# Router logits in column groups during the mixer, a gather into feature rows, four modulation tiles in the second block, and another chain behind the experts

## What is computed

```python
x = x + ada_x[2][:, None, :] * yx                                # end of the mixer
hx2 = modulate(rmsnorm(x, norm_ffn_g[l]), ada_x[3], ada_x[4])    # h * (1 + scale) + shift
aff = softmax((h @ w_router).astype(float32), axis=-1)           # 16 experts
gate, idx = lax.top_k(swapaxes(aff, 1, 2), cap)                  # cap = 32 tokens of each expert
xg = h[bidx, idx]
a, b = xg @ w1[e], xg @ w3[e]
ye = ((silu(a) * b) @ w2[e]) * gate[..., None]
x = x + ada_x[5][:, None, :] * zeros_like(h).at[bidx, idx].add(ye)
x = rmsnorm(x, final_norm_g)                                     # end of the first block
ada = silu(c) @ w_ada[l] + b_ada[l]                              # second block, l = 0, 1
h = rms_norm(x, norm_mix[l]) * (1.0 + sc_m) + sh_m
... = split(h @ w_in[l])
```

## Time and profile before

| | |
|---|---|
| runs | 2255.99, 2257.81, 2257.02 us; median 2257.02 |
| profiled execution | 2254.84 us, of it 2253.0 in the span |
| mean granted TensorE clock | 0.927 |
| busy | PE 1889.1, PEld 1264.7, DVE 744.3, ACT 334.6 us |
| chain that ended last | PE 59%, DMA 33%, DVE 4%, ACT 2% |
| moved | 648.82 MB, mean 288 GB/s |

### The profile page before, as it was taken

The page is one execution under the profiler, slowest core; times in us unless marked ns, Lnnn a source line. Parts: engine busy times, 40 slices in busy tenths (PEclk is TensorE's granted clock), DMA queues, the critical chain, the costliest instruction groups (busy, mean ns, idle before and its releaser), DMA issues.

```text
span 2253.0 us, 29442 instructions
## 1 busy us (share of the span) xinstructions
PE 1889.1 (84%) x12382; PEld 1264.7 (56%) x12382; DVE 744.3 (33%) x1716; ACT 334.6 (15%) x759; POOL 0.2 (0%) x4
## 2 busy tenths in 40 slices
PE   7999989866666666666666679999999999999999
PEld 4788778411111111111111138868889978688899
DVE  3666243200000000000000034662656546725554
ACT  4132121200000000000000020360110102602100
POOL 0000000000000000000000000000000000000000
PEclk9999999987888878787888899999999999999999
DMA  9356679999999999999999994524645555246441
GB/s 327 114 210 239 224 254 357 405 428 428 428 429 428 429 428 428 428 428 428 428 428 429 428 377 168 186 75 164 230 168 183 186 179 183 76 168 241 152 169 57
DMA packets 148022, 648.82 MB, mean 288 GB/s; under 512 B 10660, under 2 KB 17425, under 8 KB 123158
## 3 DMA queue, kind: packets, MB, share of 16 engines
q1 hardware_dynamic: 144124, 643.78, 72.1%
q10 hardware_dynamic: 3802, 3.65, 0.5%
HBM read 646.36 MB, written 1.05 MB: 287 GB/s over the span
## 4 chain that ended last, share of the span: by engine, by line
PE 59%; DMA 33%; DVE 4%; ACT 2%; issue 1%; SPq 0%; ACTq 0%; DVEq 0%
DMA ring<-in_w_exp 33%; PE bank L2086 15%; PE bank L922 13%; PE bank L2769 6%; PE bank L1869 4%; PE bank L1606 4%; PE bank L2684 3%; PE bank L1884 2%; PE bank L936 1%; PE bank L965 1%; PE bank L800 1%; PE bank L1533 1%; DVE scr L2595 1%; PE bank L963 1%; PE bank L451 1%
## 5 line engine op out<-in xcount | busy, mean ns | idle before, releaser
L1869 PE MATMUL bank<-ring,arena 128*32 128x512 f32 x1968 | 305.2, 754 | 207.9 <-DMA ring<-in_w_exp 197.5
L1869 PEld LDWEIGHTS bank<-ring,arena 128*32 128x32 f32 x1968 | 60.9, 124 | 433.4 <-DMA ring<-in_w_exp 313.5
L922 PE MATMUL bank<-hx,ring 128*128 128x256 f32 x1344 | 293.0, 379 | 0.7 <-ACT hx L818 0.7
L922 PEld LDWEIGHTS bank<-hx,ring 128*128 128x128 f32 x1344 | 254.6, 190 | 37.5 <-issue 3.4
L1884 PE MATMUL bank<-ring,arena 128*32 128x512 f32 x1008 | 161.0, 781 | 78.9 <-DMA ring<-in_w_exp 67.9
L1927 DVE COPY arena<-bank 128x256 f32<-128x256 f32 x16 | 6.8, 425 | 527.2 <-PE bank L1874 527.2
L2086 PE MATMUL bank<-arena 128*128 128x256 f32 x672 | 151.0, 379 | 0.2 <-DVE arena L2135 0.2
L1884 PEld LDWEIGHTS bank<-ring,arena 128*32 128x32 f32 x1008 | 32.9, 132 | 188.7 <-DMA ring<-in_w_exp 107.8
L2086 PEld LDWEIGHTS bank<-arena 128*128 128x128 f32 x672 | 127.0, 190 | 17.5 <-DVE arena L2135 0.6
L1934 DVE COPY arena<-bank 128x256 f32<-128x256 f32 x16 | 6.8, 424 | 344.6 <-PE bank L1758 344.6
L2086 PE MATMUL bank<-ring,hx 128*128 128x256 f32 x448 | 105.8, 379 | 0.0
(11 more groups left out here) (494 smaller groups left out, 2291.2 us busy)
## 6 DMA issues: line engine op xcount, KB each, us to landing
ring<-in_w_exp SPq DMA_DIRECT2D x186, 2048.0 KB, 16.3
ring<-in_w_ada SPq DMA_DIRECT2D x36, 2048.0 KB, 12.8
ring<-in_w_in SPq DMA_DIRECT2D x29, 2048.0 KB, 8.9
ring<-in_w_ffn_in SPq DMA_DIRECT2D x20, 2048.0 KB, 8.0
ring<-in_w_ffn_out SPq DMA_DIRECT2D x10, 2048.0 KB, 7.8
ring<-in_w_out SPq DMA_DIRECT2D x6, 2048.0 KB, 10.8
arena<-in_w_exp SPq DMA_DIRECT2D x4, 2048.0 KB, 19.0
ring<-in_w_up_nsa SPq DMA_DIRECT2D x2, 2048.0 KB, 7.9
```

The costliest lines, as they stand in the source:

```text
L922: ins = pe.matmul(b[:, o:o + n], w[:, k, j * P:(j + 1) * P], h[:, k, :], start=k == 0, stop=k == KD - 1)
L1869: ins = pe.matmul(banks[s][32 * j:32 * j + 32, :], e_xe[:, 2 * t + kk, :], w[:, kk, 512 * j:512 * j + 512], start=t + kk == 0, stop=t + kk ...
```

## The change

- The logits are made from the unnormed xT with gained weights, four chunks at a time in four column groups, the first four during the mixer's output; four partial sums are added when they are turned to tokens. The norm's factor is applied per token behind, by sums of squares with the squares as weights and two columns of ones. Constants of the shift are made early.
- The gather takes token rows as weights and e_ps as the moving side, so that features come out on partitions; ACT's copy and the turn fall away and DVE adds the shift.
- The pairs -2 and -1 leave the router's stage. Pair -2 now stands behind input tile 0 of layer 0; each layer has a pair inside its attention. The pairs are numbered 4l-2 to 4l+1.
- Tiles 4 to 7, 10 and 11 of the first expert have the places outside the ring; 0 to 3 are in the ring, 8 and 9 wait for 0 and 1.
- The last expert is written out of the loop; it has no next gather, its last tile comes in two halves, and its scatter is waited for by pairs of chunks.
- The join makes one norm factor per token from squares as weights and two columns of a weighted vector, spreads it by a diagonal matrix and a matmul, and does the final norm (two matmuls on pre-added squares, `pe_fin`) behind input tile 0.

```diff
     tiles("out1_", wide(A["w_out"][0], 0, D))
-    tiles("late-2_", later[16:18])
-    tiles("late-1_", later[18:20])
     N_PRE = len(stream)
...
-               + wide(w2, QB0, MERGE2))
+        w_first = (wide(w2, 0, KW0) + [(w2[:, KW0:QB0].rearrange("(k p) n -> p k n", p=P), P, KD, QB0 - KW0)]
+                   + wide(w2, QB0, MERGE2))
+        if l:
+            late_tiles(4 * l - 2)
+        for t, ap in enumerate(w_first):
+            after_experts.append((f"in{l}_{t}", ap))
+            if t + l == 0:
+                late_tiles(4 * l - 2)
         merge = wide(w2, MERGE2, IN2)
         for t in range(4):
             if t == 2:
...
+        pe.wait_ge(*at("join weights"))
+        b = bank(pe, "join g")
+        for k in range(KD):
+            pe.wait_ge(*at(f"join square{k}"))
+            for c in range(NC):
+                ins = pe.matmul(b[:, 2 * c:2 * c + 2], sqx[:, k, c * P:(c + 1) * P], j_w[:, k, :], start=k + c == 0, stop=True,
+                                skip_group_check=True)
+        ins.then_inc(*PE.step("full join g"))
+        b = bank(pe, "join scale")
+        for c in range(NC):
+            pe.wait_ge(*at(f"join diagonal{c}"))
+            ins = pe.matmul(b[:, c * P:(c + 1) * P], ones[:, 0:P], j_diag[:, c, :], start=True, stop=True)
+        ins.then_inc(*PE.step("full join scale"))
+
+    def pe_fin(pe):
+        PE.stage("join")
+        pe.wait_ge(*at("fin squares"))
+        b = bank(pe, "join x")
+        for k in range(2):
+            ins = pe.matmul(b[:, 0:N], ones[:, 0:P], sqx[:, k, :], start=k == 0, stop=k == 1)
+        ins.then_inc(*PE.step("full join x"))
+        PE.stage("second")
...
+            act.activation(sqx[:, k, :], xT[:, k, :], ACT.Square).then_inc(*AC.step(f"join square{k}"))
+        act.wait_ge(*at("join eps"))
+        act.wait_ge(*at("full join g"))
+        act.activation(j_root, bank_of("join g")[:, 0:4:2], ACT.Sqrt, bias=j_eps[:, 1:2]).then_inc(
+            *AC.step("free join g", "join root"))
...
+        v.wait_ge(*at("join root"))
+        v.reciprocal(j_rs, j_root).then_inc(*DV.step())
+        v.wait_ge(*DV.last())
+        for c in range(NC):
+            v.tensor_scalar(j_diag[:, c, :], ident[:, :], j_rs[:, c:c + 1], None, ALU.mult).then_inc(*DV.step(f"join diagonal{c}"))
+        v.wait_ge(*at("full join scale"))
         for k in range(KD):
-            v.tensor_tensor(sqx[:, k, :], xT[:, k, :], xT[:, k, :], ALU.mult).then_inc(*DV.step(f"join x square{k}"))
-        v.tensor_tensor(g_join, gs, c_fin[:, 0:8], ALU.mult).then_inc(*DV.step())
...
+            v.scalar_tensor_tensor(sqg[:, k, :], xT[:, k, :], g_join[:, k:k + 1], bank_of("join scale")[:, 0:N], ALU.mult,
+                                   ALU.mult).then_inc(*DV.step("free join scale", f"join scaled{k}"))
+        v.tensor_tensor(sqx[:, 0:4, :], sqx[:, 0:4, :], sqx[:, 4:8, :], ALU.add).then_inc(*DV.step("join halves"))
+        v.wait_ge(*at("join halves"))
+        v.tensor_tensor(sqx[:, 0:2, :], sqx[:, 0:2, :], sqx[:, 2:4, :], ALU.add).then_inc(*DV.step("fin squares"))
...
+                pe_linear_T(pe, f"mixout{p}{t}", f"{wo}{t}", merged, N, 4, None if t else f"merged{p}",
+                            (lambda j: pe_route_early(pe, 4 * t + j)) if p == 0 else None)
...
+    def dve_route_early(v):
+
+        dve_gain(v, "gain ffn0", gs, c_ffn[:, 0:8], adaX[0][:, 32:40], "adaX0b")
+        DV.stage("route")
+        v.wait_ge(*K.loaded("load_moe"))
+        v.wait_ge(*at("full mturn1"))
+        v.memset(e_wrg[:, :, EXPERTS:CAP], 0.0).then_inc(*DV.step())
+        v.tensor_tensor(e_wrg[:, :, 0:EXPERTS], e_wr, spread(gs, 2, EXPERTS), ALU.mult).then_inc(*DV.step("router gained"))
+        v.tensor_tensor(e_wsh, e_wr, spread(adaX[0][:, 24:32], 2, EXPERTS), ALU.mult).then_inc(*DV.step())
+        v.wait_ge(*DV.last())
+        v.tensor_reduce(e_ws, e_wsh.rearrange("p k e -> p e k"), AX, ALU.add).then_inc(*DV.step("router shift"))
+        v.memset(e_eps, EPS).then_inc(*DV.step("eps"))
+        v.memset(e_y, 0.0).then_inc(*DV.step("y zero"))
...
+            DV.stage("route")
+        for k in ((), (1,), (2, 3), (4, 5))[i]:
+            v.wait_ge(*at(f"route square{k}"))
+            if k > 1:
+                v.wait_ge(*DV.last())
+            v.tensor_tensor(e_sq[:, 0, :], e_sq[:, 0, :], e_sq[:, k, :], ALU.add).then_inc(*DV.step("squares summed"))
...
+    def pe_route_logits(pe, r):
+        PE.stage("route")
+        if r == 0:
+            pe.wait_ge(*at("router gained"))
+        for q in range(4):
+            k = 4 * r + q
+            pe.wait_ge(*at(f"x mixed0 {k}"))
+            ins = pe.matmul(bank_of("logits")[32 * q:32 * q + 32, 0:N], e_wrg[:, k, :], xT[:, k, :], start=r == 0, stop=r == 1)
+        ins.then_inc(*PE.step("full logits"))
...
+    def pe_route_early(pe, j):
+
+        stage = PE.cur
+        PE.stage("route")
+        if j == 0:
+            pe.wait_ge(*at("router shift"))
+            b = bank(pe, "router shift")
+            pe.matmul(b[:, 0:EXPERTS], ones[:, 0:P], e_ws, start=True, stop=True)
...
+            ins.then_inc(*PE.step("full router shift"))
+            book.bank["logits"], book.bank["token sums"] = 6, 7
+            claim(pe, 6, "logits")
+            claim(pe, 7, "token sums")
+        elif j == 1:
+            pe_rope(pe)
+        elif j == 5:
+            pe_route_logits(pe, 0)
+        PE.cur = stage
...
+        sums = bank_of("token sums")
+
+        def squares(n, k):
+            for c in range(NC):
+                ins = pe.matmul(sums[:, 2 * c:2 * c + 2], e_sq[:, k, c * P:(c + 1) * P], ones[:, 0:2], start=n + c == 0,
+                                stop=True, skip_group_check=True)
+            return ins
+
+        pe.wait_ge(*at("squares summed"))
+        squares(0, 0)
+        pe_route_logits(pe, 1)
+        for n, k in ((1, 6), (2, 7)):
+            pe.wait_ge(*at(f"route square{k}"))
+            ins = squares(n, k)
+        ins.then_inc(*PE.step("full token sums"))
+        pe.wait_ge(*at("logit parts"))
+        book.bank["ltok"] = 6
+        b = claim(pe, 6, "ltok")
...
-        for c in range(NC):
-            for j in range(4):
-                ins = pe.matmul(banks[2][32 * j:32 * j + 32, 0:256], e_ps[:, c, :], e_htok[:, c, 256 * j:256 * j + 256],
-                                    start=c == 0, stop=c == NC - 1)
+        for t in range(4):
+            for kk in range(2):
+                o = banks[2][:, (2 * t + kk) * CAP:(2 * t + kk + 1) * CAP]
+                for c in range(NC):
+                    ins = pe.matmul(o, e_htok[:, c, 256 * t + kk:256 * (t + 1):2], e_ps[:, c, :], start=c == 0, stop=c == NC - 1)
         ins.then_inc(*PE.step(f"{name}gathered"))
 
...
+    def dve_gathered(v, name):
+
+        v.wait_ge(*at(f"{name}gathered"))
+        v.tensor_tensor(e_xe, banks[2][:, 0:256].rearrange("p (k s) -> p k s", k=KD), spread(e_shp, 2, CAP), ALU.add).then_inc(
+            *DV.step(f"{name}xe"))
 
...
-                w = tile(8 + t, 4, D)
+                if last and t == 3:
+                    pe.wait_ge(K.sem("tile_half"), 16)
+                    w = place(EXP0 + 11, P, 4, D)
+                else:
...
+            if last:
+                PE.stage("last")
+                pe.wait_ge(*at("last G"))
+                for j in range(KD):
+                    pe.wait_ge(*at(f"last y{j // 4}"))
+                    ins = pe.matmul(banks[4 + j // 2][:, (j % 2) * N:(j % 2 + 1) * N], e_y[:, j * P:(j + 1) * P], e_G,
+                                        start=False, stop=True, skip_group_check=True)
+                    ins.then_inc(*PE.step(f"last scattered{j}"))
+                return
...
+        def last():
+            DV.stage("last")
+            v.wait_ge(*at("gathered", back=1))
+            v.tensor_scalar(e_row, e_pa, ident[0:EXPERTS, EXPERTS - 1:EXPERTS], None, ALU.mult).then_inc(*DV.step("last row"))
...
+            v.wait_ge(*at("b full"))
+            v.tensor_tensor(e_h, e_h, banks[1][:, :], ALU.mult).then_inc(*DV.step("last h ready"))
+            dve_gain(v, "gain mix1", gs, c_mix2[:, 0:8], adaX[1][:, 8:16], "ada20")
+            v.tensor_tensor(g_join, gs, c_fin[:, 0:8], ALU.mult).then_inc(*DV.step())
...
+            v.wait_ge(*at(f"last scattered{j | 1}"))
...
+                if l == 0 and t == 0:
+                    pe_fin(pe)
+                    pe_late(pe, 4 * l - 2)
+                    PE.stage("second")
...
+        pe_late(pe, 4 * l - 1)
...
-        pe_late(pe, 3 * l + 1)
+        pe_late_turn(pe, 4 * l - 1)
+        pe_late(pe, 4 * l)
...
         sp.wait_ge(*at("z2"))
-        extra_tile(0)
-        extra_tile(1)
+        extra_tile(4)
+        extra_tile(5)
         sp.wait_ge(*at("full merge07"))
-        one(N_PRE - 4, stream[N_PRE - 4])
-        one(N_PRE - 3, stream[N_PRE - 3])
-        extra_tile(2)
-        extra_tile(3)
+        extra_tile(6)
+        extra_tile(7)
         sp.wait_ge(*at("merged0 done7"))
-        extra_tile(4)
-        one(N_PRE - 2, stream[N_PRE - 2])
```

(20 more changed lines are left out.)

339 lines of the change are left out of this document (189 added, 150 removed).

## The result

| | before | after |
|---|---|---|
| median of the runs | 2256.27 us | 2263.64 us |
| range (7 runs each) | 2255.99 to 2257.81 | 2259.41 to 2265.68 |
| profiled execution (span) | 2254.84 (2253.0) | 2263.64 (2261.9) |
| mean granted clock | 0.927 | 0.907 |
| PE busy | 1889.1 | 1951.9 |

The ratio is 1.0029, 95% interval 1.002 to 1.0039: slower, by more than the 0.2% that can be told from no change. I had forecast 2244.8, and the range 2236 to 2252.5 does not hold the result.

The account below looks back on a forecast made before the run. It took the stream of expert tiles to bound the span: its start, a fixed number of tiles, and what follows. Stream -9.9, join -11.6 and second block +9.3 gave -12.2, so 2244.8 us, range 2236 to 2252.5.

Parts of the forecast that it names:

- the second dip: Expert tile stream: a new standstill until expert 1 has used its first tile, ended by an issue at 444.4.
- input stage to tile 2, added: Second block's input stage: final norm's sums 0.9, an uncovered late pair 3.7, a wait behind input tile 3 of 0.3.
- two attentions, added: Second block: one more late pair in each of two attentions, 2.2 us each, 4.4 together.
- Part 1: Router: first expert matmul at 408.2, 6.6 us earlier, with the new gather at 3.75 us (bounds 1.1 to 7).
- Part 2: Expert stream: from 444.4, restart 2.7 plus 176 tiles of 4.90, last tile at 1310.0; a gain of 9.9 us.
- plus a fixed number of tiles: Expert stage: once going for good, the stream takes 4.90 us for each of a set count of tiles (176, 862.4 us).
- Part 3: Join, from the last expert tile to the second block's first matmul: 9.8 us instead of 21.4, gain 11.6 (bounds 9 to 12.5).
- Part 4: Second block, where PE is the path: final norm, late pairs and a wait behind tile 3 give back 9.3 us.
- the open pair: Second block's input stage: a late pair that the join no longer hides adds 3.7 us.
- The stall behind tile 3: Second block's input stage: input tile 3, sent when late tile 0 is used, makes PE wait for DVE, 0.3 us more.
- Rival 4: Input stage starts at the low TensorE clock after a thin join, doubling work; gain gone at 12.2 us; chance 0.05.
- Rival 3: Router: stream starts no earlier as output blocks slip; first expert near 415, last tile 1317, 2255.5 in all; chance 0.06.

Follow-up runs that it names:

- e2: Changed kernel plus two dense 128x512 matmuls of zeros on PE ahead of its wait for the router's slots; 2258.51 us, ratio 1.0011 to the kernel before.
- e5: Changed kernel with the gather's weights taken as 128 neighbouring columns instead of every second one (output wrong, same work); 2263.49 us, ratio 1.0028.
- e9: Changed kernel with the loop's new gather moved from behind the last w2 tile to behind the second and third, 16 records each; 2256.53 us, ratio 0.9995.
- e4: Kernel before with only the new gather form, in router and loop, without ACT's copy and PE's turn; 2274.77 us, ratio 1.0076.
- e1: Changed kernel with the old gather form, ACT's copy and PE's turn put back in router and loop; 2248.59 us, ratio 0.9962.
- e7: e3 plus four dense 128x256 matmuls into an unused bank between the join's small matmuls; 2245.05 us, ratio 0.9953.
- e3: Changed kernel with both the old gather form (e1) and the two dense matmuls in the router (e2); 2245.22 us, ratio 0.9948.
- e6: Changed kernel with late pair -2 moved from layer 0's input tiles into its attention, behind unit 3, pair -1 behind unit 5; 2258.27 us, ratio 1.0011.
- e10: Changed kernel with the gather between tiles (e9), dense fills in router and join, and both late pairs in layer 0's attention; 2246.97 us, ratio 0.996.
- e8: Changed kernel with old gather, dense fills in router and join, and late pair -2 in layer 0's attention; 2243.24 us, ratio 0.9944.

## Why the prediction was wrong, point by point

| step | forecast | measured |
|---|---|---|
| top-k starts | 396.8 | 396.72 |
| first expert matmul (Ts) | 408.2 | 411.11 |
| the issue that ends the second dip | 444.4 | 451.4 |
| stream from there to the last half tile (E) | 865.6 | 875.6 |
| E | 1310.0 | 1326.99 |
| E to the input stage | 9.8 | 11.6 |
| input stage to tile 2, added | 4.9 | 7.6 |
| two attentions, added | 4.4 | 3.9 |

The sum was -12.2; the rows that went astray are 17.0 + 1.8 + 2.7 - 0.5 = 21.0; the span grew by 8.9 (-12.2 + 21.0 = 8.8).

**Part 1** was right up to the gather, to within 0.2 us, and wrong at it. So close an agreement is luck in part: in the traces of e2, e5 and e9, whose kernels are unchanged up to there, the same turn of the slots stands 0.9 to 1.6 us later. I had bounded the gather by 1.1 and 7 and took 3.75, the row of the same shape, which had been recorded at the high clock. That the upper bound met the 7.01 is luck too: its 0.22 a record came from sums with 256 columns moving, and not from a low clock. The step that failed is that I let that row stand without asking what PE does ahead of it. The same change that put the gather there took away the late pair, so PE idled 2.30 us and the clock went to half. Measured: 7.01 at 0.50, 4.52 in e2 at 0.84, 3.93 in e4 at 1.00. The Trainium skill, "TensorE: Matmul & The Clock Gate", section "LDWEIGHTS (loading the stationary operand)", gives 107 ns for 128 columns; the trace comes near it with 123 ns a record at clock 1.00 (3.93 / 32), not with 219 at 0.50 (7.01 / 32).

**Part 2** had the second dip, and its size was off by 7.0: 2.9 from Ts, 2.8 from the first four tiles at half clock (9.89 against 7.08), and 1.3 from more of the same at 434 to 438. Then it failed outright: "plus a fixed number of tiles". I held the loop to be full at 4.90 a tile, whatever PE does, since PE is at 6 tenths there. That is true on the average only. What the stream needs is that no stretch without a tile given back outlasts the three other tiles less the 2.4 us of a restart. I had counted the gather once for the first expert and once for the second dip, and never for the fourteen turns in between, where it costs nothing in eight and 1.1 to 2 us in six. e1 and e9 show it: 10 us. The gathers of the loop stand right behind waits for tiles, and in six of the fourteen turns they ran at the low level from the start. In the other eight they took 4.0 to 4.7 us, and then the scatter behind them took 5.0 to 6.5, where it took 3.7 to 4.1 in e1: behind the new gather the clock was lower even where the gather itself began at the high level. The changed kernel's page groups the gathers (count | busy us, mean ns | idle before):

```profile
L1862 PE MATMUL bank<-arena,hx 128*128 128x32 f32 x512 | 88.4, 343 | 0.6 <-DVE arena L1944 0.6
```

That is 5.5 us for each of 16 gathers, between 3.96 (at 441.80, clock 1.00) and 7.04 (at 496.94). The Trainium skill, the same page, section "HAM oscillation — how this bites in real kernels", describes waits for DMA between groups of matmuls that throw PE back to the low clock; the rows at 494.32 to 503.79 agree (a wait of 2.97 us, then 7.04 us for the gather). Not every such wait does it here: behind another of 2.97 us, at 554.87, a tile took 1.92 us, as at the high level.

**Part 3** was right in its mechanism: the join lost 9.7 of 21.4 us, and I said 11.6. The term that was too small is the sums of squares, which I had ending at E + 7.1, close behind ACT; their 32 records began only when the scatter was through and took 3.64 us at clock 1.00 (the row at 1331.55), to E + 8.2. The matmuls that spread the scale (1.20 us, where I allowed 0.4) make up the rest. My low bound, 9, was for matmuls at half clock; the clock was 1.00 from 1330 to 1335 and 0.50 from 1335 to 1340.

**Part 4**: the final norm (1.03) and the open pair (3.7) cost what I said. The stall behind tile 3 was 1.55 and not 0.3, since the tile landed at 1366.2 and DVE then had two sums to make, and the first input tile took 15.58 instead of 13.97 because the clock was low at its start (e7 shows this: 14.08 with PE busy ahead). The attention of layer 0 took 3.4 more, of which 1.37 is a gap in the middle of the late pair that no row explains; that of layer 1 took 0.5. Without such a gap, in e3, layer 0 took 1.8 more (103.7 against 101.95).

**The rivals.** Rival 4 had the right mechanism at the wrong place: I looked for the lowered clock in the input stage, where it cost 1.6, and not at the gather, where it cost most. Rival 3 was nearest in E (1317), still 10 short of 1327.0, and for a reason that did not occur: the output blocks didn't slip. No case had a loss inside the loop, and this is why the range was too narrow: its far end, 2252.5, is 11 us short. The gather of 7 us was among my bounds, but I had priced it at 6 us in all. I had given slower a chance of 0.04. Even that isn't consistent: it puts 0.03 of rival 4's 0.05 beyond the bound, while rival 4 says that two thirds of it fall short.

## What to carry to other kernels

Where a ring of n buffers feeds a stream that sets the time, ask of every edit in the loop: how long is the longest stretch in which no buffer is given back, and is it shorter, at the low clock too, than n - 1 transfers less the time that a dry stream needs to get going again? An engine that is 70% busy (590 of 840 us here) can still starve the stream; work that was put between two waits for tiles was free in the loop (e9), and the same work behind the last tile was not. And take the duration of a matmul or weight load only from a row whose preceding stretch is as busy as the new place will be: taking filler work away, as here the late pairs, can halve the clock of what follows. Here 1.9 us of dense work that computes nothing brought the gather from 7.01 to 4.52 us and the median down by 5.

## What the runs showed of the hardware

- A float32 product with 128 weight columns and few moving ones takes a time that goes by its weights: with 32 columns moving 0.12 us a record at clock 1.00 (3.93 us for 32) and 0.22 at 0.50, and with 2 columns moving still 0.11 at 1.00 (3.64 for 32). With 32 weight columns and 256 moving ones, in four column groups, 16 records took 1.05 to 1.07 at the high level. A stride of two in the weights makes no difference that can be seen (1.0028 and 1.0029).
- Behind 32 such records the clock was low even where they began at the high level: 0.57 over 416 to 420 in e4, 0.50 over 409.5 to 414 in e2. The idle time before the first tile was 0.93 us in e4 and 0.87 in the kernel before, so it hardly explains e4. What brought the clock down in e1 and e3, where the old gather stood at this place, was not tried.
- The ring's reserve: three tiles, 14.7 us, less some 2.4 us from a request to the full rate. Stretches of 12.8 to 13.2 us, and 1.8 more, lost 1.1 to 2.0 us of transfer in each of six turns; those of 9.0 to 10.7, and 1.8 more, lost next to nothing in this trace, and e1's 6.2 nothing.
- A late pair in an attention that waits for DVE costs 0.5 us (layer 1), 1.8 (e3) or 2.0 (each of the two in e6) instead of its 3.7, where it has no gap inside.
- The gap inside a late pair of layer 0's attention stands in six of the ten profiles of kernels with such a pair: 1.35 to 1.66 us in the changed kernel, e2, e5, e9 and e10, 2.08 in e8, none in e1, e3, e6 and e7. Its cause was not tried and stays open.
